# FFN layers three and four: the up blocks of seven pairs with 512 moving columns, their sums added by VectorE

## The reference, cut to what matters

```
def conv_glu(hn, w_in, conv_w, conv_b, w_out):
    u, gate_in = jnp.split(hn @ w_in, 2, axis=-1)
    c = (conv_w[0] * shift_right(gate_in, 2) + conv_w[1] * shift_right(gate_in, 1)
         + conv_w[2] * gate_in + conv_b)
    return (jax.nn.gelu(c, approximate=False) * u) @ w_out
```

## Time and profile before

| | |
|---|---|
| median of 3 timed runs | 1286.54 us (1286.2 to 1286.6) |
| the profiled execution, first to last instruction (its span) | 1284.3 us |
| median less span | 2.2 us |
| TensorE busy with matmuls / weight loads | 98% / 96% of the span |
| VectorE / ScalarE busy | 71% / 59% |
| matmuls | 12162 |

### The profile page before, as it was taken

The page is one execution under the profiler, slowest core; times in us unless marked ns, Lnnn a source line. Parts: engine busy times, 40 slices in busy tenths (PEclk is TensorE's granted clock), DMA queues, the critical chain, the costliest instruction groups (busy, mean ns, idle before and its releaser), DMA issues.

```text
span 1284.3 us, 29209 instructions
## 1 busy us (share of the span) xinstructions
PE 1264.3 (98%) x12162; PEld 1232.1 (96%) x12162; DVE 917.8 (71%) x1314; ACT 756.7 (59%) x980; POOL 41.2 (3%) x34
## 2 busy tenths in 40 slices
PE   9999999999999999998999999999999999999997
PEld 8999999998999999998989899999999889999997
DVE  5779887488569887478757388665588779666557
ACT  6667665367657665367555266554475876554444
POOL 1010000010010000000000010000001001000000
PEclk9999999999999999999999999999999999999999
DMA  8465555555345555545401136555534335555520
GB/s 343 170 225 182 202 189 209 189 191 210 119 156 190 197 196 197 196 158 196 165 34 41 64 140 230 196 195 197 187 141 176 132 128 208 198 196 196 196 99 34
DMA packets 31980, 220.61 MB, mean 172 GB/s; under 512 B 3712, under 2 KB 3840, under 8 KB 6160
## 3 DMA queue, kind: packets, MB, share of 16 engines
q1 hardware_dynamic: 30672, 213.36, 46.2%
q0 software_dynamic: 784, 4.85, 1.1%
q10 hardware_dynamic: 432, 1.05, 0.2%
HBM read 218.20 MB, written 1.05 MB: 171 GB/s over the span
## 4 chain that ended last, share of the span: by engine, by line
PE 84%; DVE 9%; ACT 4%; issue 1%; DMA 1%; POOL 0%; SPq 0%; DVEq 0%; ACTq 0%; POOLq 0%
PE ps L1915 21%; PE ps L1917 21%; PE ps L1916 21%; PE ps L1926 16%; DVE w_lo L1127 3%; PE ps L1921 2%; PE ps L1923 2%; PE ps L1922 2%; ACT w_hi L507 1%; DVE xt L1179 1%; PE ps L2140 1%; DVE xA L1190 1%; DMA raw<-stream 1%; DVE xB L1151 0%; DVE xB L1190 0%
## 5 line engine op out<-in xcount | busy, mean ns | idle before, releaser
L1127 DVE TENSOR_TENSOR w_lo<-raw,w_hi 128x2048 fp32r<-128x2048 f32 x197 | 449.6, 2288 | 137.4 <-ACT w_hi L507 137.2
L507 ACT ACTIVATE w_hi<-raw 128x2048 fp32r<-128x2048 f32 x197 | 376.3, 1914 | 157.7 <-PE ps L1917 152.0
L1915 PE MATMUL ps<-xB,w_hi 128*128 128x256 f32 x1120 | 311.0, 278 | 0.5 <-DVE w_lo L1127 0.5
L1916 PE MATMUL ps<-xB,w_hi 128*128 128x256 f32 x1120 | 309.3, 276 | 0.0
L1917 PE MATMUL ps<-xB,w_lo 128*128 128x256 f32 x1120 | 309.2, 276 | 0.0
L1915 PEld LDWEIGHTS ps<-xB,w_hi 128*128 128x128 f32 x1120 | 210.2, 188 | 2.1 <-issue 1.5
L1915 PE MATMUL ps<-xA,w_hi 128*128 128x256 f32 x744 | 208.9, 281 | 2.1 <-DVE gl L1540 1.6
L1916 PEld LDWEIGHTS ps<-xB,w_hi 128*128 128x128 f32 x1120 | 210.3, 188 | 0.1
L1917 PEld LDWEIGHTS ps<-xB,w_lo 128*128 128x128 f32 x1120 | 210.3, 188 | 0.0
L1917 PE MATMUL ps<-xA,w_lo 128*128 128x256 f32 x744 | 205.7, 276 | 0.0
L1916 PE MATMUL ps<-xA,w_hi 128*128 128x256 f32 x744 | 205.7, 276 | 0.0
(11 more groups left out here) (317 smaller groups left out, 1847.8 us busy)
## 6 DMA issues: line engine op xcount, KB each, us to landing
raw<-stream SPq DMA_DIRECT2D x199, 1024.0 KB, 4.8
raw<-stream SPq DMA_DIRECT2D x4, 512.0 KB, 7.4
at_bias<-rel POOLq DMA_DIRECT2D x1, 2048.0 KB, 8.3
hT<-x_t SPq DMA_DIRECT2D x4, 256.0 KB, 6.0
lora_w<-lora POOLq DMA_DIRECT2D x1, 1024.0 KB, 5.1
out_t<-xt SPq DMA_DIRECT2D x4, 256.0 KB, 2.6
hcon<-hyc POOLq DMA_DIRECT2D x1, 576.0 KB, 3.9
wsT<-wst ACTq DMA_DIRECT2D x1, 512.0 KB, 4.8
```

What stands on the lines that cost most here:

```text
L507: nc.scalar.activation(w_hi[c.slot][:], raw[c.slot][:], ACT.Copy).then_inc(hi_made, 1)
L1127: nc.vector.tensor_tensor(w_lo[c.slot][:], raw[c.slot][:], w_hi[c.slot][:].bitcast(F32), ALU.subtract).then_inc(lo_made, 1)
L1915: nc.tensor.matmul(out, wh, xh, start=start, stop=False, skip_group_check=True)
L1916: nc.tensor.matmul(out, wh, xl, start=False, stop=False, skip_group_check=True)
```

## The change

It concerns f = 2 and 3 alone, and there the up chunks of pairs 2 to 8. `split_chunk` takes the place of `wide_chunk`: for each k and b, one matmul of the upper weights over the upper and the lower x together (512 columns, which fill a whole bank), and one of the lower weights over the upper x (256 columns) added into the bank's first half. The two blocks now need two banks, 2·par and 4 + par. The two halves of each bank must be added: VectorE does so in `product` with a `tensor_reduce` for each block before the multiplication, which then reads the sum out of `up_acc`; it waits for its own two reduces by the new semaphore `up_summed`. TensorE waits once in each layer for `rs_made`, before pair 2 writes bank 4. Pairs 9 and 10 stay as they were, since `down` takes banks 4 and 5 next, and are written out on TensorE and VectorE, so that the loop there has three rounds.

```diff
-                def product(q, par):
+                def product(q, par, split=False):
...
+                        if split:
+                            for b, bank in enumerate((2 * par, 4 + par)):
+                                nc.vector.tensor_reduce(up_acc[par][:, b, :],
+                                                        ps[:, bank, :].rearrange("p (i t) -> p t i", i=2),
+                                                        AX_X, ALU.add).then_inc(up_summed, 1)
+                            dve.wait_ge(up_summed, q * 2 + (14 * (f - 2) - 2))
+                            up = up_acc[par][:]
                     nc.vector.tensor_tensor(up_acc[par][:], up, gate_acc[par][:], ALU.mult).then_inc(prod_made, 1)
...
+            def split_chunk(c, banks, x):
+
+                pe.wait_ge(lo_made, c.count(1))
+                for k in range(KD):
+                    for b, bank in enumerate(banks):
+                        wh, wl = weight(c, 2 * k + b)
+                        plain(ps[:, bank, :], wh, x[:, k].rearrange("p i t -> p (i t)"), k == 0, False)
+                        last = plain(half(bank, 0), wl, x[:, k, 0, :], False, k == KD - 1)
+                last.then_inc(chunk_used, 1)
...
-                    wide_chunk(cu, 2 * par, x, ready)
+                    if split:
+                        split_chunk(cu, (2 * par, 4 + par), x)
+                    else:
+                        wide_chunk(cu, 2 * par, x, ready)
...
-                pair(2, 0, Chunk(c0 + 4), Chunk(c0 + 5))
-                with pe.Fori(0, (PAIRS - 3) // 2) as it:
+                if not both:
+                    pe.wait_ge(rs_made, n + 1)
+                pair(2, 0, Chunk(c0 + 4), Chunk(c0 + 5), split=not both)
+                with pe.Fori(0, (PAIRS - 3) // 2 - (not both)) as it:
                     for j in range(2):
-                        pair(it * 2 + (3 + j), (3 + j) % 2, Chunk(c0 + 6 + 2 * j, it), Chunk(c0 + 7 + 2 * j, it))
+                        pair(it * 2 + (3 + j), (3 + j) % 2, Chunk(c0 + 6 + 2 * j, it), Chunk(c0 + 7 + 2 * j, it),
+                             split=not both)
+                if not both:
+                    pair(9, 1, Chunk(c0 + 18), Chunk(c0 + 19))
+                    pair(10, 0, Chunk(c0 + 20), Chunk(c0 + 21))
```

More of the change, by code:

```diff
@@ L283, in build @@
         gate_on = sem("gate_on")
+        up_summed = sem("up_summed")
         prod_made = sem("prod_made")
@@ L1259, in rest_hid, with pair @@
                                             ALU.subtract).then_inc(hid_lo, 1)
-                def pair(q, par, cu, cg, first=False, second=False):
+                def pair(q, par, cu, cg, first=False, second=False, split=False):
                     product_first = second and f == 2
@@ L1275, in pair @@
                     if not (first or product_first):
-                        product(q - 1, 1 - par)
+                        product(q - 1, 1 - par, split)
                     if not (first and f == 2):
@@ L1286, in ffn @@
                 pair(2, 0, Chunk(c0 + 4), Chunk(c0 + 5))
-                with dve.Fori(0, (PAIRS - 3) // 2) as it:
+                with dve.Fori(0, (PAIRS - 3) // 2 - (not both)) as it:
                     for j in range(2):
-                        pair(it * 2 + (3 + j), (3 + j) % 2, Chunk(c0 + 6 + 2 * j, it), Chunk(c0 + 7 + 2 * j, it))
+                        pair(it * 2 + (3 + j), (3 + j) % 2, Chunk(c0 + 6 + 2 * j, it), Chunk(c0 + 7 + 2 * j, it),
+                             split=not both)
+                if not both:
+                    pair(9, 1, Chunk(c0 + 18), Chunk(c0 + 19), split=True)
+                    pair(10, 0, Chunk(c0 + 20), Chunk(c0 + 21))
                 product(PAIRS - 1, (PAIRS - 1) % 2)
@@ L2038, in ffn, with pair @@
                 up_used = up_conv if both else prod_made
-                def pair(q, par, cu, cg, ready=None):
+                def pair(q, par, cu, cg, ready=None, split=False):
                     if ready is None:
                         pe.wait_ge(up_used, q + (base - 1))
-                    wide_chunk(cu, 2 * par, x, ready)
+                    if split:
+                        split_chunk(cu, (2 * par, 4 + par), x)
+                    else:
+                        wide_chunk(cu, 2 * par, x, ready)
                     if ready is None:
```

## The result

| | before | after |
|---|---|---|
| median of 8 timed runs | 1286.37 us | 1289.67 us |
| lowest to highest | 1284.91 to 1286.60 | 1287.96 to 1291.41 |
| span of the profiled execution | 1284.3 us | 1286.2 us |
| TensorE matmuls | 12162 | 11938 |

A forecast was written before the change was run, and what follows sets the result against it. The prediction took TensorE's matmul distances as the bound. Matmul pairs 1.0 ns cheaper than threes gave -0.2 us, and VectorE's hidden work and the rest nothing: 1286.54 - 0.2 = 1286.3 us, range 1284.1 to 1288.4.

The forecast's parts named there:

- What bounds the kernel: Third and fourth layers' up chunks: TensorE never idle, time is the number of matmuls times their distance, 113.3 ns each.
- the price of the new pair of matmuls: Split chunks: 512 plus 256 columns take 339.0 ns instead of 340.0 for three matmuls, 0.2 us less in all.
- the turned form: Existing matmuls with x loaded and weights moving: 230.4 ns for 512 columns, 118.0 for 256; their difference priced the change.
- C: Rival on split chunks: the new order meets the turned form's extra, +0.8 to +1.9 us, 1287.3 to 1288.4; chance 0.17.
- its end of 348.4: Upper bound for a wide and a narrow matmul, 230.4 + 118.0 ns: +8.4 ns each, +1.9 us in all.
- 215 to 231: Sign on split chunks: a wide matmul's distance outside this range, in ns, would show the prediction wrong.
- A: Forecast for split chunks: time goes with columns, total moves at most 0.8 us either way, 1285.7 to 1287.3; chance 0.50.
- B: Rival on split chunks: wide matmul pays a per-matmul or per-load part once, -1.1 to -2.6 us, 1283.9 to 1285.5; chance 0.27.
- the delay: VectorE in each split pair: two reduces and a wait put the product back by 1.5 us, hidden by idle time.
- the idle time left: VectorE ahead of the convolution in each split pair: 2.0 us of idle time would remain after the reduces.
- D: Rival on VectorE: slow crosswise reduces make it the pair's bound, 18 us slower, about 1304.5; chance 0.04.

The follow-up runs named there:

- the grid: Kernel of matmuls alone against the whole kernel, lower weights and x each at 16 offsets, 0 to 240 bytes; no place gave less than 340.0 ns for either form.
- its part alone: Changed kernel with each 512-column matmul given as two of 256, keeping both banks, the reduces and all new VectorE work; ratio 1.0008.
- the last pair of runs: Kernels before and after the change, both with pads of 64 bytes ahead of the lower weights and 224 ahead of x: 1318.35 and 1315.09 us.

## Why the prediction was wrong

- What bounds the kernel: right. TensorE is never idle in either layer, and the time is the sum of distances.
- The failed step is the price of the new pair of matmuls, "on our 113.3 this gives 225.7 ns, and 339.0 for the pair of matmuls". It measured 353.3, +13.3 in place of -1.0, and with what the first matmuls save and the gate chunk pays +3.2 us in place of -0.2. I took the surplus of the turned form (118.0 for 113.3) as a trait of that form which a difference would cancel. But about 118 is the usual state of this form too (median of 256 places), and 113.3 is the exception, held here only by 256 columns after 256 columns. The difference itself held: in the split chunk 233.3 - 120 = 113.3 for the 256 further columns, and what was wrong is the state that it was put on. (That the turned form's 118.0 has the same cause is likely and was not tried.) A difference of two rows out of one state cannot be put on a row out of another.
- The trace of before had the hint. The same form, x moving, can leave its beat for a while after an irregularity. Its early matmuls of the third layer, behind two that came after 172 and 222 ns:

```profile
767.32 0.40 PE L1926 MATMUL ps<-xB,w_lo 128*128 128x256 f32 x2
767.56 0.63 PE L1926 MATMUL ps<-xB,w_hi 128*128 128x256 f32 x4
768.03 0.40 PE L1926 MATMUL ps<-xB,w_lo 128*128 128x256 f32 x2
768.27 0.51 PE L1926 MATMUL ps<-xB,w_hi 128*128 128x256 f32 x3
```

  From 767.32 to 768.27 there are 8 matmuls in 0.95 us, 118.8 ns each; behind 768.4 they are back at 113.3. It doesn't come after every irregularity: behind the wait of 0.48 us at 776.62 the beat was back after two matmuls. Read in time, this would have given C a row of our own form, and more than 0.17.
- The bounds: C, "what is loaded beside what moves does matter", was the right mechanism at 0.17, but its end of 348.4 was too low. It took the two surpluses from one place of the turned form; the grid reaches 366.8 for a three and 363.4 for the two, and has 353.4 for the two at the kernel's own place. The wide matmul's 233 ns also lies outside the 215 to 231 that I had named as a sign of being wrong.
- A and B: both wrong here. Two matmuls below 340.0, as B needs, appear at none of 256 places, and at the kernel's own the time goes with the state, not with the columns.
- VectorE: right. A reduce took 683 ns (taken as 0.69), the delay 1.3 us (1.5), the idle time left 2.4 (2.0), and its part alone costs nothing from pair 2 on. D is excluded.
- The rule of the page "TensorE: Matmul & The Clock Gate" (section "Back-to-back issue gap") would have given 325.0 for the two. By this rule nothing here fits: 340.0 is the least in 256 places. The page gives this formula for the gap of an isolated matmul, without a budget for its load, and every matmul here has a load. The Trainium skill says on the same page, section "Step-by-step: what each phase is for", that loading the next tile's weights doesn't steal read bandwidth of SBUF from the running matmul; no run here shows which of the two reads yields, but that distances depend on where both lie, with all else at rest, is shown.

Open is the mechanism in the array: that the load and the moving data meet in SBUF would fit the period of 256 bytes in x and the beat, but was not isolated, since a matmul without its load was not tried.

## What to carry to other kernels

Before merging matmuls to save loads or instructions, read the distance from start to start in several states, after a wait and in mid-stream: if a form has two distances, the lower one may hang on equal widths and on the place of the operands, and another sequence may fall back to the higher. A change to such a stream is judged together with the offsets of its tiles, and a sweep by matmuls alone does this in one run: here it foretold 3.0 us less at another place, and 3.0 us less came. Where work ahead wanders by tenths of a microsecond, as here, measure from the first instruction that the change touches. A cost that a bound takes from a like form must come from the same state.

## What the runs showed of the hardware

- The distance of `fp32r` matmuls of 256 columns depends on the byte offsets between upper weights, lower weights and x modulo 256: 113.3 ns at 5 of 256 places, a mean of 117 to 120 at 237 of them, with a median of 117.8. 32 bytes more ahead of x made the changed kernel take 1321.1 us (one run) in place of 1289.67.
- At the kernel's place a matmul of 512 columns among those of 256 takes 226 ns if it comes out of the even beat, and 229 to 236 in most others; four matmuls of 256 columns restore the beat after one wide one, and some fifteen after sixteen wide ones. At the place of the last pair of runs wide and narrow ones hold an even beat of their own, 227 and 113 ns.
- VectorE's `tensor_reduce` over pairs 1 KB apart in PSUM takes 683 ns for 512 values read and 256 written, as long as a product of 512.
